# Hiding two RMS norms behind matrix products: the FFN norm at a change of phase, and the last norm inside the last down projection

## The reference, cut to what matters

```python
def _rmsnorm(x, w):
    x32 = x.astype(jnp.float32)
    y = x32 * lax.rsqrt(jnp.mean(x32 * x32, axis=-1, keepdims=True) + RMS_EPS)
    return (y * w.astype(jnp.float32)).astype(x.dtype)
...
    out = (g_ssd * y_ssd + g_hgrn * y_hgrn) @ lw["w_out"]
...
    x = x + g_m * mix
    h = _rmsnorm(x, lw["norm_ffn_w"]) * (1 + sc_f) + sh_f
    ffn = (jax.nn.silu(h @ lw["ffn_w1"]) * (h @ lw["ffn_w3"])) @ lw["ffn_w2"]
    x = x + g_f * ffn
...
    y_prompt = _rmsnorm(ctx, norm_final_w)
    y_sample = _rmsnorm(lat, norm_final_w)
```

## Time and profile before

| what | value |
|---|---|
| median of the timed runs | 3182.78 us |
| the profiled execution's own time | 3179.53 us |
| its span, first to last instruction | 3177.7 us |
| TensorE busy | 3081.7 us, 97% of the span |
| VectorE, ScalarE, GpSimd busy | 48%, 39%, 23% |
| mean granted TensorE clock | 0.985 of full speed |

### The profile page before, as it was taken

How to read it: one execution, slowest core, us unless ns; L and a number is a source line. 1 busy time by engine, 2 the same in 40 slices (tenths; PEclk the granted TensorE clock), 3 DMA queues, 4 the chain that set the end, 5 groups by cost and what they waited for, 6 DMA issues and landing times. The chain is left out here.

```text
span 3177.7 us, 59794 instructions
## 1 busy us (share of the span) xinstructions
PE 3081.7 (97%) x22144; PEld 2952.3 (93%) x22144; DVE 1540.5 (48%) x2645; ACT 1230.5 (39%) x2339; POOL 728.4 (23%) x911
## 2 busy tenths in 40 slices
PE   6999999999999999999999979999989999999996
PEld 4799999999999999999999979999889999999996
DVE  3546747567466575675756333443343222222233
ACT  6346455454554555545556332212331102211213
POOL 0013535245253362444524500001200000000000
PEclk8999999999999999999999989999999999999998
DMA  7522222122231221312212344433211111111112
GB/s 258 208 87 74 80 74 83 40 81 79 64 95 40 82 77 47 108 44 78 79 48 75 96 136 143 136 94 87 77 33 40 42 47 44 40 40 44 42 37 76
DMA packets 287487, 250.56 MB, mean 79 GB/s; under 512 B 11304, under 2 KB 259216, under 8 KB 287248
## 3 DMA queue, kind: packets, MB, share of 16 engines
q1 hardware_dynamic: 250752, 197.07, 20.0%
q10 hardware_dynamic: 36496, 50.35, 5.0%
HBM read 210.90 MB, written 36.47 MB: 78 GB/s over the span
## 5 line engine op out<-in xcount | busy, mean ns | idle before, releaser
L750 PE MATMUL bank<-h_hi,w_hi 128*128 128x384 f32 (+1 forms) x2520 | 877.5, 348 | 9.6 <-DVE w_lo L1370 9.6
L750 PE MATMUL bank<-h_hi,w_lo 128*128 128x384 f32 (+1 forms) x2520 | 845.2, 335 | 0.0
L750 PE MATMUL bank<-h_lo,w_hi 128*128 128x384 f32 (+1 forms) x2520 | 844.7, 335 | 0.0
L2024 PE MATMUL bank<-a_hi,v_hi 128*128 128x384 f32 x1440 | 490.4, 341 | 30.3 <-DVE a_lo L2235 12.4
L750 PEld LDWEIGHTS bank<-h_hi,w_hi 128*128 128x128 f32 (+1 forms) x2520 | 472.7, 188 | 26.7 <-DVE w_lo L1370 9.8
L2024 PE MATMUL bank<-a_lo,v_hi 128*128 128x384 f32 x1440 | 485.7, 337 | 0.0
L2024 PE MATMUL bank<-a_hi,v_lo 128*128 128x384 f32 x1440 | 485.6, 337 | 0.0
L750 PEld LDWEIGHTS bank<-h_lo,w_hi 128*128 128x128 f32 (+1 forms) x2520 | 473.2, 188 | 3.9
L750 PEld LDWEIGHTS bank<-h_hi,w_lo 128*128 128x128 f32 (+1 forms) x2520 | 472.4, 187 | 1.3
L1848 POOL TENSOR_TENSOR kq<-kq,fg 128x384 f32<-128x384 f32 x288 | 289.3, 1034 | 177.6 <-PE bank L879 145.4
L2024 PEld LDWEIGHTS bank<-a_hi,v_hi 128*128 128x128 f32 x1440 | 273.4, 190 | 43.0 <-issue 32.5
(11 more groups left out here) (266 smaller groups left out, 4058.4 us busy)
## 6 DMA issues: line engine op xcount, KB each, us to landing
raw<-in_w_in SPq DMA_DIRECT2D x104, 512.0 KB, 4.0
cumb<-cum_scratch SPq DMA_DIRECT2D x72, 512.0 KB, 6.2
raw<-in_ffn_w SPq DMA_DIRECT2D x60, 512.0 KB, 3.8
ada_late<-in_ada_w SPq DMA_DIRECT2D x8, 2048.0 KB, 8.6
small<-gate_scratch ACTq DMA_DIRECT2D x72, 192.0 KB, 2.4
gate_scratch<-th ACTq DMA_DIRECT2D x48, 192.0 KB, 1.9
y_scratch<-x_t SPq DMA_DIRECT2D x8, 1152.0 KB, 4.8
small<-y_scratch ACTq DMA_DIRECT2D x48, 192.0 KB, 2.5
```

What stands on the lines that cost most here:

```text
L750: last = pe.matmul(out, w[i][:, k, 0:cols_n], h[:, k, blk(hb)], start=(k == 0 and j == 0), stop=(k == KT - 1 and j == 2))
L2024: last = pe.matmul(banks[3 * s + b][:, 0:BW], wp[s][:, k, :], operand[ap][:, k, blk(b)], start=(k == 0 and j == 0), stop=(k == kt - 1 and ...
```

## The change

In short:

- The residual of `o` comes in one DMA of 4608 KB from `x_scratch` straight to `x_acc`, issued by ACT once all parts of `h` are made; DVE's additions of `o` wait for it (`x_back`). The 24 loads of 192 KB go.
- The last round of `o`, the first of `up0` and the last of `down2` run block by block: (0,0), (1,0), (0,1), (1,1), (0,2), (1,2) (`TURNED`).
- The FFN norm of a block starts when both of its products of the last `o` round are added. The product with ones of blocks 0 and 1 stands inside the products (0,1) and (0,2) of that round, that of block 2 behind the first product of `up0`. The eight steps of a block's norm are interleaved by hand with the additions and the weights on DVE and ACT.
- All rounds of `down2` also square their tiles (ACT) and add them up (POOL). In the last round PE makes the sums of a chunk's squares by products with one column of ones, ACT takes a square root, DVE a reciprocal, PE transposes the chunks between products, and DVE scales them to `x_acc` (or `raw`, for the last two), from where SP stores them. `last_norm` goes.

The diff, cut to its core:

```diff
+TURNED = [(s, b) for b in range(NB) for s in range(2)]
+NORM_AT = 5
+PAIRS = ((6, 7), (0, 3), (6, 7), (0, 3), (1, 4), (6, 7), (0, 3), (1, 4), (6, 7))
...
 # SyncE
+            sp.wait_ge(parts, PARTS["down2"] + NB * HCH[2])
+            sp.dma_start(w_all, m["norm_final_w"]....broadcast_to([P, KT, P])).then_inc(w_here, 16)
+            for c in range(NC):
+                sp.wait_ge(scaled_out, 2 * (c + 1))
...
+                sp.dma_start(dst.rearrange("p (k n) -> p k n", n=P), rows_out(c)[:, :, :]).then_inc(rows_moved[c], 16)
...
 # TensorE
+            def ones_product(b):
+                pe.wait_ge(sq_added, 19 + 2 * (b + 1))
...
+                for k in range(kt):
+                    if k == NORM_AT and norm is not None:
+                        ones_product(norm)
...
+            def add_squares(b):
+                pe.wait_ge(sq_done, SQ_BEFORE + 18 + 2 * b + 2)
+                pe.wait_ge(sq_added, ADD_BEFORE + 3 + 18 + b + 1)
+                for j in range(CB):
+                    pe.matmul(banks[3 + b][:, j:j + 1], tmp[b][:, chunk(j)], ones[:, 0:1], start=True, stop=False)
+                    last = pe.matmul(banks[3 + b][:, j:j + 1], stage[b][:, chunk(j)], ones[:, 0:1],
+                                     start=False, stop=True)
+                last.then_inc(ms_done, 1)
+            def tail():
+                for b in range(NB):
+                    unit("down2", 3, 0, b)
+                    if b > 0:
+                        add_squares(b - 1)
+                        for c in ((0, 1), (3, 4, 5))[b - 1]:
+                            turn_back(c)
+                    unit("down2", 3, 1, b)
+                    if b == 1:
+                        turn_back(2)
+                turn_back(6)
+                turn_back(7)
+                add_squares(2)
+                turn_back(8)
...
 # ScalarE
+            def turn():
+                I = it("o", 3)
+                high(1, I)
+                square(3, 0, 0)
+                square(3, 1, 0)
+                rstd(0)
+                square(3, 0, 1)
+                normed(0, range(0, 3))
+                square(3, 1, 1)
+                normed(0, range(3, 5))
+                square(3, 0, 2)
+                normed(0, range(5, 7))
+                high(2, I, UNITS + 5)
+                normed(0, (7,))
+                rstd(1)
+                square(3, 1, 2)
+                high(1, I + 1)
+                normed(1, range(KT))
+                rstd(2)
+                normed(2, range(KT))
...
+                    act.wait_ge(parts, PARTS["up"])
+                    act.dma_start(x_acc[:, :, :], x_dram.rearrange("k p t -> p k t")).then_inc(x_back, 16)
...
 # VectorE
+            def add_product(name, i, s, b):
+                if name == "o":
+                    dve.wait_ge(x_back, 16)
...
+            def turn():
+                I = it("o", 3)
+                low(1, I)
+                for s, b in TURNED[0:3]:
+                    add_product("o", 3, s, b)
+                normed(0, range(0, 3))
+                add_product("o", 3, 1, 1)
+                normed(0, range(3, 5))
+                add_product("o", 3, 0, 2)
+                normed(0, range(5, 7))
+                low(2, I)
+                normed(0, (7,))
+                add_product("o", 3, 1, 2)
+                low(1, I + 1)
+                normed(1, range(KT))
+                normed(2, range(KT))
...
+            def scale_out(c):
+                dve.wait_ge(turned_back, c + 1)
...
+                for j in range(2):
+                    ks = slice(4 * j, 4 * j + 4)
+                    dve.scalar_tensor_tensor(rows_out(c)[:, ks, :],
...
+            def tail():
+                low(1, it("down2", 3))
+                for s, b in TURNED[0:3]:
+                    add_product("down2", 3, s, b)
+                rstd_last(0)
+                scale_out(0)
+                scale_out(1)
+                add_product("down2", 3, 1, 1)
+                scale_out(2)
+                add_product("down2", 3, 0, 2)
+                rstd_last(1)
+                for c in (3, 4, 5):
+                    scale_out(c)
+                add_product("down2", 3, 1, 2)
+                rstd_last(2)
+                for c in (6, 7, 8):
+                    scale_out(c)
```

More of the change, by code:

```diff
@@ L176, in build @@
         m_w_in = [sem(f"m_w_in{i}") for i in range(2)]
+        rows_moved = [sem(f"rows_moved{c}") for c in range(NC)]
         with ExitStack() as keep_h:
@@ L1962, in mod_col, with rows_out @@
         return mod[:, bass.ds(t + j, 1), who:who + 1].rearrange("p a b -> p (a b)")
+    def rows_out(c):
+        return x_acc[:, :, chunk(c)] if c < NC - 2 else raw[c % 2]
     with nc.Block() as block:
@@ new lines, in unit @@
+                for k in range(kt):
+                    if k == NORM_AT and norm is not None:
+                        ones_product(norm)
+                    if s == 0 and name in ("s1", "up0"):
+                        pe.wait_ge(parts, (0 if name == "s1" else PARTS["up"]) + b * KT + k + 1)
+                    for j, (wp, ap) in enumerate(((w_hi, 0), (w_hi, 1), (w_lo, 0))):
+                        last = pe.matmul(banks[3 * s + b][:, 0:BW], wp[s][:, k, :], operand[ap][:, k, blk(b)],
+                                         start=(k == 0 and j == 0), stop=(k == kt - 1 and j == 2))
@@ L2013, in body @@
+                last.then_inc(unit_done, 1)
+            def body(name, i):
                 for s in range(2):
-                    pe.wait_ge(w_split, I * 2 + (s + 3))
                     for b in range(NB):
[L2017 to L2027, removed]
+                        unit(name, i, s, b)
@@ new lines, in turn_back @@
+            def turn_back(c):
+                base, b = it("down2", 3) * UNITS + UNITS, c // CB
+                if c in (1, 4):
+                    pe.wait_ge(root_done, b + 1)
+                elif c > 0:
+                    pe.wait_ge(scaled_out, 2 * (c - 1 if c < 4 else c - 2) if c > 2 else 2)
+                for k in range(KT):
+                    if k == 0:
+                        pe.wait_ge(freed, base + 2 * b + 1)
+                    elif k == KT - 1:
+                        pe.wait_ge(freed, base + 2 * b + 2)
+                    last = pe.transpose(banks[PAIRS[c][k // 4]][:, (k % 4) * P:(k % 4 + 1) * P],
+                                        x_acc[:, k, chunk(c)], ident)
+                last.then_inc(turned_back, 1)
@@ L2029, in _ @@
             for name, n in PHASES:
-                with pe.Fori(0, n) as i:
-                    body(name, i, False)
                 if name == "o":
[L2033 to L2038, removed]
+                    with pe.Fori(0, n - 1) as i:
+                        body(name, i)
@@ new lines, in _ @@
+                    for s, b in TURNED:
+                        unit(name, n - 1, s, b, {(0, 1): 0, (0, 2): 1}.get((s, b)))
+                elif name == "up0":
+                    for s, b in TURNED:
+                        unit(name, 0, s, b)
+                        if (s, b) == (0, 0):
+                            ones_product(2)
+                    with pe.Fori(1, n) as i:
+                        body(name, i)
+                elif name == "down2":
+                    with pe.Fori(0, n - 1) as i:
+                        body(name, i)
+                    tail()
+                else:
+                    with pe.Fori(0, n) as i:
+                        body(name, i)
@@ L2049, in body @@
+            def tail():
+                high(1, it("down2", 3))
+                for b in range(NB):
+                    square_last(3, 0, b)
+                    if b == 2:
+                        root(1)
+                    square_last(3, 1, b)
+                    if b != 1:
+                        root(b)
             def body(name, i, last_it):
```

294 lines of the change are left out of this document (160 added, 134 removed).

## The result

The changed kernel takes 3159.5 us (median of four, 3156.2 to 3161.8) against 3182.97 for the kernel before, now the median of four runs: a ratio of 0.9926, with a 95% interval of 0.9911 to 0.9941. The forecast was 3155.9, its range 3149 to 3168. The profiled execution of after took 3156.18 us (span 3154.4), 23.4 less than that of before, where the sum said 26.9.

What follows compares the result with a forecast made beforehand. TensorE, busy 97% of the span, bounds the kernel, so only its standing or the time behind its last product can give. 20.3 + 15.1 - 8.5 = 26.9 us; 3182.78 - 26.9 = 3155.9 us, range 3149 to 3168.

Steps and rivals of the forecast that it cites:

- Part 1: FFN norm inside the rounds of `o` and `up0`: twelve products in 59.8 us instead of 80.1, gain 20.3.
- The standing until (0,2) is done: Wait within block 0's FFN norm until product (0,2) of `o`, with its product with ones, ends: about 1.1 us.
- The drain behind a table load: FFN norm on ACT: the skill's 1.38 us after each table switch, not counted; with it the gain would be 14.8, not 20.3.
- Part 2: Residual of `o` in one DMA: landing at 2204.4, PE stands 6.8 us, slow matmuls cost 1.7; loss 8.5 us.
- the write in the other direction: Basis for the residual load's time: the same 4608 KB between the same forms of tile and buffer took 13.6 us.
- the slow read: Rival for the residual load: it comes at `ada_late`'s rate, 19.4 us instead of 13.6, time 3161.7; chance 0.13.
- the landing at 55.8: Rival for the residual load: slowest load's rate, landing 55.8 us after issue, 3197.6 us, slower than before; chance 0.04.
- Part 3: Last norm inside `down2`'s last round: 39.9 or 40.0 us from that round's start to the end against 55.1, gain 15.1.
- The slow clock: Rival in `down2`'s last round: mixing transposes, tiny matmuls and products drops PE's clock; some 3173 us; chance 0.08.
- H: Start of `h`'s last low part, a moment used to cut the profiles; the forecast had no term for it.

Runs made afterwards that it cites:

- ACT's order: Kernel after, with ACT's Ln and Exp of block 1 ahead of the square of (0,2), and the high part ahead of that of (1,2): 3156.72 us.
- the two partial kernels: Kernel before with only the last norm changed: 3166.27 us; with only the FFN norm and the residual load changed: 3171.12 us.

## Why the prediction was right, and where it was off

- Part 1, 20.3 forecast, 18.8 measured in the profile of after and 17.2 where the clock fell. From the start of the round (2273.65) block 0's norm starts at 14.4 (14.6 forecast, though the forecast's own terms add up to 14.4) and ends at 30.6 (29.1); all that follows is later by the same 1.5: block 1 starts at 35.3 (33.8), block 2 ends at 56.5 (55.0). The mis-sized term is the length of block 0's norm, 16.2 us where 14.5 were forecast. The standing until (0,2) is done, taken as 1.1, was only 0.78 (a row above). Two things came out larger. ACT stands at each square until DVE's addition, and then DVE waits for ACT's next piece, 0.62 and 0.63, where the 11.2 taken from before holds two such waits of 0.21: 0.8 more. And three places of DVE's norm are longer where they lie beside an addition of POOL: the first scalings 2.17 (1.41 in the earlier trace rows) and two pairs of low parts 0.89 and 0.91 (0.73 elsewhere): 1.1 more. Together that is the difference, to 0.1 us. The rows, DVE's two waits and then POOL's additions:

```profile
2295.35 0.89 DVE L2328 SCALAR_TENSOR_TENSOR a_lo<-small,mod,a_hi 128x128 fp32r<-128x128 f32 x2 [0.62 <-ACT a_hi L2167]
...
2300.24 0.91 DVE L2328 SCALAR_TENSOR_TENSOR a_lo<-small,mod,a_hi 128x128 fp32r<-128x128 f32 x2 [0.63 <-ACT a_hi L2167]
```

```profile
2288.54 1.17 POOL L2483 TENSOR_TENSOR small<-small 128x384 f32<-128x384 f32 x1 [3.92 <-ACT small L2154]
2294.71 0.99 POOL L2483 TENSOR_TENSOR small<-small 128x384 f32<-128x384 f32 x1 [5.00 <-ACT small L2154]
2299.59 1.01 POOL L2483 TENSOR_TENSOR small<-small 128x384 f32<-128x384 f32 x1 [3.89 <-ACT small L2154]
```

- All eight profiled executions with part 1 show the same three, and before, where no step of the norm lies beside an addition of POOL, has none. With ACT's order POOL's last addition falls on block 1's first two scalings, and these take 1.89 instead of 1.14. That is a coincidence in every trace; no experiment took POOL's additions away, so the cause is argued. Also, PE stood 1.84 for the sums of block 1 where 1.3 was taken, and the price of a fallen clock there was in no term.
- The drain behind a table load that the Trainium skill ("ScalarE: Activation LUTs", What ACT_TABLE_LOAD costs) adds was not there: the load at 2302.66 takes 1.28, and Ln starts at 2303.95.

```profile
2302.66 1.28 ACT L2158 ACT_TABLE_LOAD   x1
2303.95 0.58 ACT L2158 ACTIVATE small<-bank,cst 128x384 f32<-128x384 f32 x1
```

- Part 2, 8.5 forecast, 8.8 to 10.1 measured in the five profiled executions with one load. The landing, 14.0 us after the issue in after (14.1 to 14.5 in the others), the standing of 7.0 and the slow matmuls behind it came close to what the write in the other direction gave; the slow read (19.4) and the landing at 55.8 did not come.
- Part 3, 15.1 forecast, 15.6 measured, and the nearness is partly luck: two errors cancel. The last scaling ends at 3150.41, 35.4 us from the start of the round (36.8 forecast), since a block's sums took 1.26 (1.4), a chunk's transposes 0.94 to 1.07 (1.08) and the root 0.26 (0.3). But from there to the end of the span were 4.0 us (3.1): stores of 512 KB landed after a median of 4.1 us (in pieces of 512 bytes) and 3.5 us (whole rows), where before's took 2.6. That the pieces still under way held up the last stores is likely, but not shown. The slow clock did not come: the stretch 3130 to 3140, with 32 transposes among the products, was at 1.00 in the row below (its last three numbers are the granted clock, the DMA share and GB/s). In the kernel before, behind a standing of 6.46 us, PE ran 24 transposes and nothing else from 3152.75 on, and while they ran the granted clock rose from 0.50 to 1.00 (the rows in the second fence). The Trainium skill ("TensorE: Matmul & The Clock Gate", Part 4: PE-mode transpose) says that the full clock does not engage for transposes; these rows of before do not bear that out, while the stretch of after decides nothing, since products stand beside its transposes.

```profile
3130.00:3140.00 10.00, 10.00 (x76) 9.97 (x75) 5.38 (x10) 1.30 (x3) 0.99 (x1) 1.00 0.56 159
```

```profile
3152.75 4.20 PE L2283 MATMUL bank<-cst,x_acc 128*128 128x128 f32 x24 [6.46 <-DVE out L2318]
...
3154.00:3155.00 1.00, 1.00 (x7) 1.00 (x6) 1.00 (x3) 0.25 (x1) 0.00 (x0) 0.50 1.00 397
3155.00:3156.00 1.00, 1.00 (x8) 1.00 (x7) 0.33 (x1) 0.97 (x4) 0.00 (x0) 0.71 1.01 401
3156.00:3157.00 1.00, 0.95 (x9) 0.71 (x7) 0.00 (x0) 0.88 (x5) 0.00 (x0) 1.00 0.98 393
```

- Not in the sum at all: H. Before's profiled execution had the earliest H of ten (by 0.01), and after's was 2.35 later. A sum made against one execution carries that, and of the 3.5 us by which the sum exceeded the profiles' difference it is the greater part. Why `h` and the phases ahead of it wander is only half settled: `h` wanders where DVE waits for gate loads (27.8 us of waits), and in the two executions where it waits for PE it did not.
- Open: the medians of the two partial kernels sum to a gain of 26.6, and after's was 21.6 and 23.5 in two groups. The profiles' stretches (without H) add up to within 0.6 us, so the difference would lie in H and in the fallen clock of (0,2); for the executions that have no profile this is argued, not shown.

## What to carry to other kernels

Before one transfer replaces many small ones, ask what its first reader needs: the whole residual in one load cost 9 to 10 us, and a first quarter of its own gave all of it back. When steps are interleaved by hand, durations taken from a stretch where the engines worked undisturbed can be too short: each change of hands can add a wait, and a neighbour's work beside a step may lengthen it (0.8 and 1.1 us here). Take the noise of the unchanged stretches from several profiles before reading a difference of 2 us.

## What the runs showed of the hardware that was not expected

- The same standing of PE for 1.84 us, behind the same instructions of PE, left the granted clock at 1.00 in three profiled executions and took it to its lower level in four (0.66 to 0.73 in the lowest stretch of 5 us), for a cost of 1.6 us.
- Transposes alone brought the granted clock from 0.50 to 1.00 in the kernel before (from 3154 to 3157).
- DVE's scalings and low parts beside an addition of POOL took up to 0.76 us longer, in every profiled execution with part 1.
- 3456 KB, issued 1.1 us behind 1152 KB on the same queue, landed 14.5 us after their issue, 4608 KB alone 14.0: the time of a load was not its own bytes alone.
